# Loads of the cached blocks and the first layer of their compression ahead of the projection

## The chip, the cores and the metric

The kernel runs on 1 core of one Trainium2 chip. The metric is device time in microseconds (us) of one execution; three runs are given for the kernel before. The engines are PE (matrix multiply), DVE (vector), ACT (scalar), POOL (GpSimd) and SP (the queue that issues most transfers). They run in parallel and meet at semaphores.

## What is computed

One layer of a decoder step for a prompt of 512 tokens and 8 sample tokens, 520 columns in all, width 1024:

```
m = silu(c) @ ada_w + b -> shift1, scale1, gate1, shift2, scale2, gate2
h = rmsnorm(x) * (1 + scale1) + shift1
z = h @ w_in                      -> recurrent group, queries, K/V of three branches, gates
past = cache_cmp_kv[page_table]   -> 8 sequences x 8 pages x 128 rows, K and V
hidden = sum over m of chunk_proj(past, w1)[m] + pos @ w1      (first layer)
ck = gelu(hidden) @ w2                                          (second layer)
o = gates * (attend(ck), attend(selected blocks), attend(window))
x += gate1 * concat(rmsnorm(recurrent), rmsnorm(o)) @ w_out
x += gate2 * PEER(rmsnorm(x) * (1 + scale2) + shift2);  y = rmsnorm(x)
```

The change touches the order of m, h, z, hidden and ck for the sample tokens. The formulas stay as they are.

## The kernel before

The engines' programs are written out by hand, one function for each engine; the order of the lines is the order on the engine, and on SP, POOL and ACT it is also the order in which transfers are issued. All tensors of the front section are views of one tile in SBUF, `arena`, so the profile calls most of them by that name.

**Modulation.** The matrix `ada_w` comes as 48 chunks of 512 KB. The first 16 are loaded as four parts of 2048 KB (`load_head`) and used by four wide steps (`ada_step`, L576, 512 columns each). ACT copies each result (`copy_m9`), PE turns it (`turn_m9`, L586), DVE adds the bias (`shift_m`). The other 32 chunks (`load_tail`, two buffers) are used two per piece of the projection, from piece 2 on. In between, PE sums the squares of x that ACT makes (`strip_sums`, L556) and spreads the roots (`spread_roots`, L563).

**Projection.** The loop over n from 0 to 17 (ZC is 18) multiplies one piece of 128 output features: 8 x 2 matmuls of 260 columns (L691), weights of 512 KB in two buffers (`w_in`), results in banks 0 to 3 of `ps`. DVE copies the even pieces and ACT the odd ones (`z_moved`). Piece n + 2's weights are issued when piece n is done (`z_ready`). After pieces 0 and 1 come the gate columns and the bias rows (`gate_strips`, `bias_rows`, `gate_sums`).

**Cached blocks.** `page_rows` reads a page number from SBUF and issues one load of 128 KB (128 rows of 1 KB). 64 loads fill `xpool`: blocks 0 to 19 on SP (8 before the loop, then 4 in each of the rounds 2, 3 and 4), blocks 20 to 63 on POOL, behind a wait for the third wide part. `hidden_pages` (L605) is the first layer, for keys (c = 0) and values (c = 1), 128 matmuls in the trace each, with a position sum of 64 narrow ones (L610). It stands after piece 4. Gelu follows on ACT, then the second layer (`keys_pages`, `values_pages`, L618 and L624), whose last copy piece 6 waits for.

**What else is on the queues.** In round 4 of its loop SP loads the window keys (`win_kT`, 2048 KB), in round 5 the recurrence weights (`wlru`). From round 7 on it loads three selected blocks (`pool_s`) a round into the memory of `xpool`. POOL stores the bias scratch, builds the bias tables through memory (L474 to L486), and then loads 21 selected blocks.

Behind the loop stand the attention over the caches (from L742; the first work is the transposes of L749), the prompt's attention and the feed-forward part, which takes most of the span.

## Time and profile before

| | |
|---|---|
| median of 3 runs | 1851.36 us (1847.32 to 1853.66) |
| the profiled execution's own time | 1851.92 us |
| its span, first to last instruction | 1850.1 us |
| mean granted TensorE clock | 0.963 |
| PE busy | 1755.8 us (95%) |
| DVE, ACT, POOL busy | 1317.2, 646.4, 350.5 us |
| PE's share of the chain that ended last | 83% |
| moved by DMA | 467.88 MB, mean 253 GB/s |

Times in the rows are from the span's start. In a row of a timeline stand the start, the length, the engine, the line, the operation, output<-input, the shape, the count, and in brackets how long the engine had been idle before and what released it. In tables of windows "busy (x)" comes for each engine in turn, then the granted clock of PE as a share of full speed, the mean busy share of the 16 DMA engines, and GB/s. "q1" is the queue of SP, "q0" that of POOL. A landing is the time from issue to the completion of a transfer.

### The profile page before, as it was taken

The numbers are of one execution on the slowest core, as the hardware profiler recorded it, in microseconds if no ns is written. First come the engines' busy times: TensorE is split into PE (matmuls) and PEld (weight loads), VectorE is DVE, ScalarE is ACT, GpSimd is POOL, SyncE is SP. The second block draws the span as 40 slices with busy tenths as digits, with TensorE's granted clock in tenths as the row PEclk, the third lists the DMA queues.
The fourth block names the chain that finished last, engine by engine and source line by source line (L and its number), as shares of the span: only waits on it lengthen the run. The fifth ranks groups of instructions, "written<-read, shape, count | busy, mean of one in ns | idle before, by whom it ended". The sixth has DMA issues, their size and how long they took to land.

```text
span 1850.1 us, 30371 instructions
## 1 busy us (share of the span) xinstructions
PE 1755.8 (95%) x11385; PEld 1633.9 (88%) x11385; DVE 1317.2 (71%) x2982; ACT 646.4 (35%) x1020; POOL 350.5 (19%) x390
## 2 busy tenths in 40 slices
PE   5999998789889999999999999999999999999997
PEld 3868876447789989999899999999999999999997
DVE  2102434663387789999899999994787777777776
ACT  2103422662132233334333343333333333333332
POOL 1512010000000001111233333332222222222220
PEclk8999996799899999999999999999999999999998
DMA  8948572500333226877799999999999999999992
GB/s 299 311 141 267 202 228 78 197 1 1 134 134 94 78 83 243 285 244 225 227 331 355 350 337 342 347 347 358 404 376 340 342 330 342 340 340 335 341 310 76
DMA packets 176606, 467.88 MB, mean 253 GB/s; under 512 B 20457, under 2 KB 90089, under 8 KB 174820
## 3 DMA queue, kind: packets, MB, share of 16 engines
q1 hardware_dynamic: 130532, 290.36, 45.3%
q0 software_dynamic: 45952, 175.97, 26.7%
q8 instruction: 68, 1.11, 0.2%
q14 instruction: 54, 0.44, 0.1%
HBM read 408.89 MB, written 64.17 MB: 256 GB/s over the span
## 4 chain that ended last, share of the span: by engine, by line
PE 83%; DVE 8%; DMA 3%; issue 2%; ACT 2%; POOLq 1%; POOL 0%; SPq 0%; DVEq 0%; ACTq 0%
PE ps L1064 29%; PE ps L960 25%; PE ps L691 5%; PE ps L1045 5%; PE ps L947 4%; PE ps L900 3%; PE ps L605 2%; ACT arena L1107 2%; PE ps L876 1%; PE ps L576 1%; DVE ul L1712 1%; PE ps L868 1%; DVE arena L1589 1%; DMA xT<-in_xT 1%; POOLq L281 1%
## 5 line engine op out<-in xcount | busy, mean ns | idle before, releaser
L1712 DVE TENSOR_TENSOR ul<-raw,uh 128x1024 fp32r<-128x1024 f32 x256 | 311.7, 1223 | 134.7 <-ACT uh L1107 118.2
L960 PE MATMUL ps<-hh,uh 128*128 128x392 f32 x1024 | 359.2, 351 | 5.3 <-DVE ul L1712 5.2
L960 PE MATMUL ps<-hl,uh 128*128 128x392 f32 x1024 | 350.5, 342 | 0.0
L960 PE MATMUL ps<-hh,ul 128*128 128x392 f32 x1024 | 349.5, 341 | 0.0
L1064 PE MATMUL ps<-ah,uh 128*128 128x392 f32 x1000 | 340.0, 340 | 3.0 <-DVE al L1921 3.0
L1064 PE MATMUL ps<-ah,ul 128*128 128x392 f32 x1000 | 342.1, 342 | 0.0
L1064 PE MATMUL ps<-al,uh 128*128 128x392 f32 x1000 | 341.4, 341 | 0.0
L1107 ACT ACTIVATE uh<-raw 128x1024 fp32r<-128x1024 f32 x256 | 270.2, 1055 | 123.8 <-PE ps L1064 103.6
L510 POOL DMA_INDIRECT xT<-in_u,gidx x128 | 147.5, 1152 | 584.8 <-DVE zg L1759 359.8
L510 POOL DMA_INDIRECT xT<-in_v,gidx x128 | 132.6, 1036 | 418.3 <-DVE vacc L1911 384.5
L1107 ACT ACTIVATE zbuf<-ps 128x392 f32<-128x392 f32 x128 | 63.7, 498 | 402.2 <-PE ps L960 355.5
L960 PEld LDWEIGHTS ps<-hh,uh 128*128 128x128 f32 x1024 | 193.9, 189 | 8.3 <-DVE ul L1712 6.6
L960 PEld LDWEIGHTS ps<-hl,uh 128*128 128x128 f32 x1024 | 193.9, 189 | 0.0
L960 PEld LDWEIGHTS ps<-hh,ul 128*128 128x128 f32 x1024 | 193.7, 189 | 0.0
L1064 PEld LDWEIGHTS ps<-ah,uh 128*128 128x128 f32 x1000 | 188.3, 188 | 3.3 <-issue 3.3
L1064 PEld LDWEIGHTS ps<-al,uh 128*128 128x128 f32 x1000 | 188.1, 188 | 0.0
L1064 PEld LDWEIGHTS ps<-ah,ul 128*128 128x128 f32 x1000 | 188.1, 188 | 0.0
L1911 DVE SCALAR_TENSOR_TENSOR vacc<-xT,ag,vacc 128x1024 f32<-128x1024 f32 x127 | 162.4, 1279 | 0.0
L1759 DVE CUSTOM_DVE_ANT_0 xT<-xT,hg 128x1024 f32<-128x1024 f32 x128 | 155.8, 1219 | 5.0 <-DMA xT<-in_u,gidx 5.0
L1107 ACT ACTIVATE ah<-zin 128x392 fp32r<-128x392 f32 x128 | 68.2, 533 | 227.6 <-DVE zin L1918 227.6
L691 PE MATMUL ps<-arena 128*128 128x260 f32 x576 | 135.2, 394 | 3.4 <-DVE arena L1381 2.0
L691 PEld LDWEIGHTS ps<-arena 128*128 128x128 f32 x576 | 111.3, 196 | 21.4 <-issue 4.2
(352 smaller groups left out, 2240.0 us busy)
## 6 DMA issues: line engine op xcount, KB each, us to landing
raw<-in_uT SPq DMA_DIRECT2D x128, 512.0 KB
raw<-in_v SPq DMA_DIRECT2D x128, 512.0 KB
zs<-zbuf SPq DMA_DIRECT2D x128, 196.0 KB
gw<-stage POOLq DMA_DIRECT2D x28, 896.0 KB
gr<-gw SPq DMA_DIRECT2D x32, 784.0 KB, 8.1
zin<-zs SPq DMA_DIRECT2D x128, 196.0 KB
arena<-in_ada_w SPq DMA_DIRECT2D x32, 512.0 KB, 4.6
arena<-in_w_in SPq DMA_DIRECT2D x18, 512.0 KB, 6.3
```

The lines of the kernel that those rows point to most:

```text
L510: pool.indirect_dma_start(out=gb[:, s, :], out_offset=None, in_=table, in_offset=bass.IndirectOffsetOnAxis(ap=gidx[:, n:n + 1], axis=0)).t ...
L605: mm(ps[g * HD:(g + 1) * HD, b + h, 1 - m:257 - m], w1p[:, c * 16 + m * 8 + j, :], xv[:, h, :, c, g, j, :], start=(m == 0 and j == 0), sto ...
L691: last = mm(ps[:, 2 * (n % 2) + h, 0:HALF], win_w[:, (n % 2) * KD + k, :], hT[:, k, h * HALF:(h + 1) * HALF], start=(k == 0), stop=(k == K ...
L900: last = mm(ps[:, 2 + 2 * (c % 3) + h, 0:HALF], wout[:, k, c * P:(c + 1) * P], zT[:, k, h * HALF:(h + 1) * HALF], start=(k == 0), stop=(k ...
L947: last = mm(ps[:, b + h, 0:HALF], weights[w](k), moving[m](k)[:, h * HALF:(h + 1) * HALF], start=(first and n == 0 and w == 0 and m == 0), ...
L960: last = mm(ps[:, bank, 0:DN], w[x][:, k * P:(k + 1) * P], m[:, k, G0:TOK], start=(k == 0 and x == 0 and m is hh), stop=(k == KD - 1 and x ...
L1045: last = mm(ps[:, 4 + n % 4, t * P:(t + 1) * P], oh[:, n % 6, t * P:(t + 1) * P], oh[:, n % 6, (4 + t) * P:(5 + t) * P], start=True, stop= ...
L1064: last = mm(ps[:, dc, 0:DN], w[:, q, cols], m[:, q, :], start=(first and w is uh and m is ah), stop=False)
L1107: return act.activation(out, in_, f, **kw)
L1712: tt(ul[:, i % 4, :], raw[:, i % 4, :], uh[:, i % 4, :].bitcast(F32), SUB).then_inc(S["lo_done"], 1)
L1759: dve.tensor_tensor_reduce(gb[:, n % 4, :], gb[:, n % 4, :], hg[:, :], 1.0, 0.0, MUL, ADD, zg[:, n:n + 1]).then_inc(S["ttr_done"], 1)
L1911: stt(vacc[:, :], gb[:, n % 4, :], ag[:, n:n + 1], vacc[:, :], MUL, ADD).then_inc(S["acc_step"], 1)
```

## The change

The loads of the 64 cached blocks go to three queues and to the start: SP issues 22 to 31 behind the first part and x, and 48 to 63 behind parts 1 and 2; POOL issues 0 to 15 and 32 to 47 from the start, without the wait for the third part; ACT issues 16 to 21 before its first copy. The weights `w1p` and `posp` go ahead of them. The page table is one row on SP, no longer a broadcast on POOL.

The first layer is cut into four pieces (`hidden_half(c, h)`), placed behind parts 0, 1, 2 and 3. The wide parts all use bank 6 and their turns bank 7, since banks 2 to 5 now hold the hidden sums. Gelu of both follows at once on ACT, into two tiles (`hid`, `hid2`). The second layer stands after piece 1, and piece 2 waits for its last copy. SP's loads of selected blocks begin in round 2, three a round; in round 3 SP also waits for the second layer. POOL's order is otherwise as before: scratch, bias tables, 21 selected blocks.

The diff, without the hunks of the list of semaphore names and of two counts that follow from it; lines around the changes are left out:

```diff
@@ -172,7 +172,7 @@
...
         oha = at(39321, OHA_W)
-        hid = at(40345, 546)
+        hid, hid2 = at(40345, 546), at(6800, 512)
         ckT = at(40891, 544)
@@ -291,17 +291,26 @@
...
+            def load_pages(a, b, s):
+                for n in range(a, b):
+                    page_rows(sp, xpool[:, n, :], io["pool_c"], n, s)
+            load(pgi[0:1], io["page_table"], S["page_loaded"])
             load(cT, io["cT"], S["c_loaded"])
...
             load(xT[:, :, :], io["xT"], S["x_loaded"])
+            load(w1p, io["w1p"], S["w1k_loaded"])
+            load(posp, io["posp"], S["w1k_loaded"])
+            sp.wait_ge(S["page_loaded"], 16)
+            load_pages(22, 32, S["half_k"])
             load(par[:, 0:80], io["par"], S["tables_loaded"])
...
             load_head(2, 2)
+            load_pages(48, 64, S["gather_k"])
             sp.wait_ge(S["ada_ready"], 1)
             load_head(3, 0)
-            load(wgate, io["w_gate"], S["wgate_loaded"])
+            load(wgate, io["w_gate"], S["small_loaded"])
             load(oha[0:33], io["oha"], S["buckets_loaded"])
@@ -315,14 +324,6 @@
...
                     load(w2[g * HD:(g + 1) * HD, c, g * HD:(g + 1) * HD], io["cmp_w2"][c], S["w2_loaded"])
-            sp.wait_ge(S["page_loaded"], 16)
-            def load_pages(a, b):
-                for n in range(a, b):
-                    page_rows(sp, xpool[:, n, :], io["pool_c"], n, S["gather_k"])
-            load_pages(0, 8)
-            load(w1p, io["w1p"], S["w1k_loaded"])
-            load(posp, io["posp"], S["pos_loaded"])
@@ -334,12 +335,11 @@
...
                 load(win_w[:, (n % 2) * KD:(n % 2 + 1) * KD, :], io["w_in"][n], w_l[n % 2])
-                if 2 <= n <= 4:
-                    load_pages(4 * n, 4 * n + 4)
-                if n >= 7:
-                    sp.wait_ge(S["hid_ready"], 2)
-                    for m in range(3 * (n - 7), min(3 * (n - 6), 32)):
-                        page_rows(sp, sel[:, m, :], io["pool_s"], m, S["gather_s"])
+                sp.wait_ge(S["hid_ready"], 2)
+                for m in range(3 * (n - 2), min(3 * (n - 1), 32)):
+                    page_rows(sp, sel[:, m, :], io["pool_s"], m, S["gather_s"])
+                if n == 3:
+                    sp.wait_ge(S["ck_ready"], 2)
                 load_tail(2 * n - 4)
@@ -460,18 +460,17 @@
...
             pool.memset(ident[:, :], 0.0).then_inc(S["pool_done"], 1)
-            pool.dma_start(pgi, io["page_table"].to_broadcast([P, NB * PAGES])).then_inc(S["page_loaded"], 16)
             pool.wait_ge(S["pool_done"], 1)
...
             pool.wait_ge(S["page_loaded"], 16)
-            pool.wait_ge(S["ada_ready"], 3)
-            for n in range(20, 64):
+            for n in range(16):
+                page_rows(pool, xpool[:, n, :], io["pool_c"], n, S["half_p"])
+            for n in range(32, 48):
                 page_rows(pool, xpool[:, n, :], io["pool_c"], n, S["pages_k"])
-                if n == 44:
-                    pool.wait_ge(S["act_init"], 3)
-                    pool.dma_start(rscratch, rsb[0:NH]).then_inc(S["scratch_stored"], 16)
+            pool.wait_ge(S["act_init"], 3)
+            pool.dma_start(rscratch, rsb[0:NH]).then_inc(S["scratch_stored"], 16)
             pool.wait_ge(S["scratch_stored"], 16)
@@ -569,81 +568,93 @@
...
-                if i >= 2:
-                    pe.wait_ge(S["m9_ready"], i - 1)
+                bank = 6 if i < ADA_HEAD else 4 + i % 2
+                if i >= 1:
+                    pe.wait_ge(S["m9_ready"], i if i < ADA_HEAD else i - 1)
                 for kk in range(2):
                     for j in range(4):
-                        last = mm(ps[32 * j:32 * j + 32, 4 + i % 2, 0:width], cT[:, 2 * j + kk, :], rhs(2 * j + kk),
+                        last = mm(ps[32 * j:32 * j + 32, bank, 0:width], cT[:, 2 * j + kk, :], rhs(2 * j + kk),
                                   start=(kk == 0), stop=(kk == 1))
...
                 pe.wait_ge(S["m9_ready"], i + 1)
-                if i >= 2:
-                    pe.wait_ge(S["mt_done"], i - 1)
+                bank = 7 if i < ADA_HEAD else 6 + i % 2
+                if i >= 1:
+                    pe.wait_ge(S["mt_done"], i if i < ADA_HEAD else i - 1)
                 m9, n = (mhead, 4) if i < ADA_HEAD else (mtail, 1)
                 for q in range(n):
-                    last = mm(ps[:, 6 + i % 2, q * 9:(q + 1) * 9], m9[:, i % 2, q * P:(q + 1) * P], pick[:, 0:9], start=True, stop=True)
+                    last = mm(ps[:, bank, q * 9:(q + 1) * 9], m9[:, i % 2, q * P:(q + 1) * P], pick[:, 0:9], start=True, stop=True)
                 last.then_inc(S["mt_ready"], 1)
-            def hidden_pages(c):
-                if c == 0:
-                    pe.wait_ge(S["w1k_loaded"], 16)
-                    pe.wait_ge(S["pos_loaded"], 16)
-                    pe.wait_ge(S["gather_k"], 16 * 20)
-                    pe.wait_ge(S["pages_k"], 16 * 44)
-                    pe.wait_ge(S["z_moved"], 4)
-                else:
-                    pe.wait_ge(S["m9_ready"], ADA_HEAD + 6)
-                xv = xpool.rearrange("p (h a) (c g j n) -> p h a c g j n", h=2, c=2, g=2, n=8)
-                b = 2 + 2 * c
-                for h in range(2):
-                    for m in range(2):
-                        for j in range(8):
-                            for g in range(2):
-                                mm(ps[g * HD:(g + 1) * HD, b + h, 1 - m:257 - m], w1p[:, c * 16 + m * 8 + j, :],
-                                   xv[:, h, :, c, g, j, :], start=(m == 0 and j == 0), stop=(m == 1 and j == 7),
-                                   skip_group_check=True)
+            xv = xpool.rearrange("p (h a) (c g j n) -> p h a c g j n", h=2, c=2, g=2, n=8)
+            def hidden_half(c, h):
+                if c == 0 and h == 0:
+                    pe.wait_ge(S["w1k_loaded"], 32)
+                    pe.wait_ge(S["half_k"], 16 * 16)
+                    pe.wait_ge(S["half_p"], 16 * 16)
+                if c == 0 and h == 1:
+                    pe.wait_ge(S["gather_k"], 16 * 16)
+                    pe.wait_ge(S["pages_k"], 16 * 16)
+                for m in range(2):
+                    for j in range(8):
+                        for g in range(2):
+                            last = mm(ps[g * HD:(g + 1) * HD, 2 + 2 * c + h, 1 - m:257 - m], w1p[:, c * 16 + m * 8 + j, :],
+                                      xv[:, h, :, c, g, j, :], start=(m == 0 and j == 0), stop=(m == 1 and j == 7),
+                                      skip_group_check=True)
+                if h == 1:
+                    last.then_inc(S["hid_ready"], 1)
+            def position(c):
                 for mj in range(16):
                     for g in range(2):
-                        last = mm(ps[g * HD:(g + 1) * HD, b, 300:301], w1p[:, c * 16 + mj, :],
-                                  posp[:, c * 16 + mj:c * 16 + mj + 1], start=(mj == 0), stop=(mj == 15))
-                last.then_inc(S["hid_ready"], 1)
+                        mm(ps[g * HD:(g + 1) * HD, 2 + 2 * c, 300:301], w1p[:, c * 16 + mj, :],
+                           posp[:, c * 16 + mj:c * 16 + mj + 1], start=(mj == 0), stop=(mj == 15))
             def keys_pages():
-                pe.wait_ge(S["gelu_ready"], 1)
+                pe.wait_ge(S["gelu_ready"], 2)
                 pe.wait_ge(S["w2_loaded"], 64)
-                pe.wait_ge(S["z_moved"], 5)
+                pe.wait_ge(S["z_moved"], 1)
                 mm(ps[:, 0, 0:512], w2[:, 0, :], hid[:, 0:512], start=True, stop=True).then_inc(S["ck_ready"], 1)
...
             def values_pages():
-                pe.wait_ge(S["gelu_ready"], 2)
                 pe.wait_ge(S["ck_moved"], 1)
                 for b in range(NB):
-                    last = mm(ps[0:NCMP_S, b // 4, (b % 4) * P:(b % 4 + 1) * P], hid[:, b * 64:b * 64 + NCMP_S],
+                    last = mm(ps[0:NCMP_S, b // 4, (b % 4) * P:(b % 4 + 1) * P], hid2[:, b * 64:b * 64 + NCMP_S],
                               w2[:, 1, :], start=True, stop=True)
...
             pe.wait_ge(S["prep_done"], 3)
-            for g in range(ADA_HEAD):
-                if g == 1:
-                    pe.wait_ge(S["act_init"], 2)
-                    for k in range(KD):
-                        last = strip_sums(0, hT, k, KD)
-                    last.then_inc(S["sum_ready"], 1)
-                if g == 2:
-                    pe.wait_ge(S["rstd_ready"], 1)
-                    spread_roots(1, 0)
-                if g >= 1:
-                    turn_m9(g - 1)
+            def head_step(g):
                 pe.wait_ge(head_l[g % 3], 16 * (g // 3 + 1))
...
                 ada_step(g, lambda k: aw[:, :, k, :], 512)
-            turn_m9(ADA_HEAD - 1)
+            head_step(0)
+            turn_m9(0)
+            pe.wait_ge(S["act_init"], 2)
+            for k in range(KD):
+                last = strip_sums(0, hT, k, KD)
+            last.then_inc(S["sum_ready"], 1)
+            hidden_half(0, 0)
+            position(0)
+            head_step(1)
+            pe.wait_ge(S["rstd_ready"], 1)
+            spread_roots(1, 0)
+            turn_m9(1)
+            hidden_half(1, 0)
+            position(1)
+            head_step(2)
+            turn_m9(2)
+            hidden_half(0, 1)
+            head_step(3)
+            turn_m9(3)
+            hidden_half(1, 1)
...
-                pe.wait_ge(S["wgate_loaded"], 16)
+                pe.wait_ge(S["small_loaded"], 80)
                 pe.wait_ge(S["mt_done"], ADA_HEAD)
@@ -680,7 +691,7 @@
...
                     pe.wait_ge(S["z_moved"], n - 1)
-                if n == 6:
+                if n == 2:
                     pe.wait_ge(S["ck_moved"], 2)
@@ -693,31 +704,26 @@
...
                     gate_strips()
+                    pe.wait_ge(S["gelu_ready"], 2)
                     bias_rows()
...
                     pe.wait_ge(S["act_init"], 3)
+                    keys_pages()
                     gate_sums()
+                    values_pages()
                 if 7 <= n <= 13 and n % 2:
                     lru_gate(n, 0)
-                if n == 5:
-                    pe.wait_ge(S["gelu_ready"], 2)
                 if n >= 2:
...
                     lru_gate(n, 1)
-                if n == 5:
-                    values_pages()
                 if n == 2:
...
                         turn_m9(ADA_HEAD + i)
-                if n == 4:
-                    hidden_pages(0)
-                    hidden_pages(1)
-                    keys_pages()
             for i in (30, 31):
@@ -1116,8 +1122,12 @@
...
                     act.wait_ge(S["mt_ready"], i - 1)
-                m9, width = (mhead, 512) if i < ADA_HEAD else (mtail, P)
-                fn(m9[:, i % 2, :], ps[:, 4 + i % 2, 0:width], ACT.Copy).then_inc(S["m9_ready"], 1)
+                bank, m9, width = (6, mhead, 512) if i < ADA_HEAD else (4 + i % 2, mtail, P)
+                fn(m9[:, i % 2, :], ps[:, bank, 0:width], ACT.Copy).then_inc(S["m9_ready"], 1)
+            act.wait_ge(S["page_loaded"], 16)
+            for n in range(16, 22):
+                page_rows(act, xpool[:, n, :], io["pool_c"], n, S["half_k"])
             copy_m9(0)
@@ -1126,19 +1136,12 @@
...
-            def gelu_pages(c):
-                link(fn(hid[:, 0:256], ps[:, 2 + 2 * c, 1:257], ACT.Gelu_apprx_tanh, bias=posb[:, c:c + 1]))
-                fn(hid[:, 256:512], ps[:, 3 + 2 * c, 1:257], ACT.Gelu_apprx_tanh, bias=posb[:, c:c + 1]).then_inc(S["gelu_ready"], 1)
-            def pages_hidden():
-                for c in range(2):
-                    act.wait_ge(S["hid_ready"], c + 1)
-                    link(fn(posb[:, c:c + 1], ps[:, 2 + 2 * c, 300:301], ACT.Copy))
-                    if c == 0:
-                        gelu_pages(0)
-                act.wait_ge(S["ck_ready"], 1)
-                fn(ckT[:, 0:512], ps[:, 0, 0:512], ACT.Copy).then_inc(S["ck_moved"], 1)
-                gelu_pages(1)
+            for c in range(2):
+                act.wait_ge(S["hid_ready"], c + 1)
+                hd = (hid, hid2)[c]
+                link(fn(posb[:, c:c + 1], ps[:, 2 + 2 * c, 300:301], ACT.Copy))
+                link(fn(hd[:, 0:256], ps[:, 2 + 2 * c, 1:257], ACT.Gelu_apprx_tanh, bias=posb[:, c:c + 1]))
+                fn(hd[:, 256:512], ps[:, 3 + 2 * c, 1:257], ACT.Gelu_apprx_tanh, bias=posb[:, c:c + 1]).then_inc(S["gelu_ready"], 1)
@@ -1151,8 +1154,6 @@
...
                     copy_m9(ADA_HEAD + 2 * n - 3)
-                    if n == 4:
-                        pages_hidden()
                     if 8 <= n <= 14:
@@ -1160,6 +1161,9 @@
...
                     continue
+                if n == 1:
+                    act.wait_ge(S["ck_ready"], 1)
+                    fn(ckT[:, 0:512], ps[:, 0, 0:512], ACT.Copy).then_inc(S["ck_moved"], 1)
                 act.wait_ge(S["z_ready"], n + 1)
@@ -1179,7 +1183,7 @@
...
                     copy_m9(ADA_HEAD + 2 * n - 3)
-                if n == 5:
+                if n == 1:
                     act.wait_ge(S["ck_ready"], 2)
@@ -1382,7 +1386,8 @@
...
                 c0, n = (4 * i, 4) if i < ADA_HEAD else (i + 3 * ADA_HEAD, 1)
-                tt(mT[:, c0:c0 + n, :], ps[:, 6 + i % 2, 0:9 * n].rearrange("p (q c) -> p q c", c=9),
+                bank = 7 if i < ADA_HEAD else 6 + i % 2
+                tt(mT[:, c0:c0 + n, :], ps[:, bank, 0:9 * n].rearrange("p (q c) -> p q c", c=9),
                    par[:, ADB + c0:ADB + c0 + n].to_broadcast([P, n, 9]), ADD).then_inc(S["mt_done"], 1)
```

## Rows read from the trace of the kernel before

**Rows 1.** The page: span in 40 slices, and the chain by engine.

```profile
DMA  8948572500333226877799999999999999999992
...
PE 83%; DVE 8%; DMA 3%; issue 2%; ACT 2%; POOLq 1%; POOL 0%; SPq 0%; DVEq 0%; ACTq 0%
```

**Rows 2.** Timeline of PE, 0 to 60 us: start, us, what, count, wait before.

```profile
10.89 3.27 PE L576 MATMUL ps<-arena 128*32 128x512 f32 x16 [10.89 <-DMA arena<-in_ada_w]
19.65 3.85 PE L556 MATMUL ps<-arena,ones 128*32 128x136 f32 x64 [5.50 <-ACT arena L1107]
...
28.90 1.16 PE L563 MATMUL ps<-arena,ident 128*128 128x128 f32 x8 [2.35 <-ACT arena L1107]
...
36.27 1.92 PE L576 MATMUL ps<-arena 128*32 128x512 f32 x16
38.91 1.06 PE L586 MATMUL ps<-arena 128*128 128x9 f32 x8 [0.72 <-ACT arena L1107]
41.95 10.13 PE L691 MATMUL ps<-arena 128*128 128x260 f32 x32 [1.98 <-DVE arena L1381]
```

**Rows 3.** Timeline of PE, 60 to 160 us.

```profile
96.89 16.73 PE L605 MATMUL ps<-arena 128*64 128x256 f32 x128 [4.36 <-DMA arena<-in_pool_c]
113.44 1.99 PE L610 MATMUL ps<-arena 128*64 128x1 f32 x64
115.28 14.02 PE L605 MATMUL ps<-arena 128*64 128x256 f32 x128
...
131.05 1.13 PE L618 MATMUL ps<-arena 128*128 128x512 f32 x2
...
144.05 7.25 PE L691 MATMUL ps<-arena 128*128 128x260 f32 x32 [1.42 <-ACT arena L1107]
```

**Rows 4.** Timeline of SP's queue, 34 to 150 us: start, us, transfer, count.

```profile
41.16 8.16 SPq L282 DMA_DIRECT2D arena<-in_pool_c  x8
...
82.94 0.82 SPq L288 DMA_DIRECT2D arena<-in_ada_w  x2
83.80 0.43 SPq L288 DMA_DIRECT2D xT<-in_win_kT  x1
84.28 0.84 SPq L288 DMA_DIRECT2D arena<-in_w_in  x1
...
94.65 9.76 SPq L288 DMA_DIRECT2D arena<-in_w_in  x1
```

**Rows 5.** The load of in_w_in within 84 to 85 us: its landing.

```profile
DMA to landing us min/median/max: 13.4/13.4/13.4
```

**Rows 6.** Windows: PE, PEld, DVE, ACT, POOL; clock, DMA share, GB/s.

```profile
10.00:16.00 6.00, 3.27 (x16) 0.67 (x16) 0.00 (x0) 0.67 (x2) 0.00 (x0) 1.00 0.99 408
42.00:50.00 8.00, 8.00 (x24) 6.47 (x25) 3.02 (x7) 0.00 (x0) 4.15 (x7) 0.64 0.77 224
52.00:64.00 12.00, 12.00 (x77) 8.88 (x77) 0.70 (x1) 1.44 (x4) 5.52 (x11) 0.86 1.02 362
170.00:230.00 60.00, 59.93 (x474) 50.11 (x473) 27.63 (x94) 27.25 (x42) 0.00 (x0) 1.00 0.59 205
```

**Rows 7.** DMA queues, 83.8 to 97.7 us: packets, MB, share of 16 engines.

```profile
q1 hardware_dynamic: 830, 4.33, 77.3%
q0 software_dynamic: 549, 1.10, 24.5%
```

**Rows 8.** Timelines: POOL from 85 us, then ACT from 15 us.

```profile
87.83 4.19 POOL L478 DMA_DIRECT2D obias<-arena  x8
...
99.45 3.84 POOL L486 DMA_DIRECT2D arena<-obias  x8 [6.89 <-DMA obias<-arena]
...
134.72 0.54 POOL L282 DMA_DIRECT2D arena<-in_pool_s  x1 [0.60 <-issue]
...
15.93 3.67 ACT L1107 ACTIVATE arena<-xT 128x4160 f32<-128x4160 f32 x1 [1.11 <-DMA xT<-in_xT]
```

**Rows 9.** Timeline, 255 to 275 us: the first work behind the projection.

```profile
256.01 1.07 PE L749 MATMUL ps<-ident,arena 128*128 128x128 f32 x8
```

More of the change, by code:

```diff
@@ L780, in _ @@
             hidden_prompt(1, 7, 128)
-            pe.wait_ge(S["w1k_loaded"], 48)
+            pe.wait_ge(S["w1k_loaded"], 64)
             hidden_prompt(0, 1, 160)
```

6 lines of the change are left out of this document (3 added, 3 removed).

## Prediction

> **What bounds the kernel now.** I read the page first. PE carries 83% of the chain that ended last, so time that PE loses in this front section I take as time of the kernel. The same page shows the DMA row at its ceiling in most of the first slices [rows 1]. So the front has two limits that take turns, and the change moves work across the border between them.
>
> Then PE's timeline of the first 60 us [rows 2]: the four wide modulation parts (L576) and their turns (L586), with 10.89, 5.50 and 2.35 us of waiting before them, then projection piece 0 at 41.95. That piece takes 10.13 us where later ones take 7.25 to 7.28: the granted clock was 0.64 over 42 to 50 us [rows 6], that is mostly the lower level (1.2 GHz), after waits of 0.72 and 1.98, and rose to the upper one within the piece.
>
> Then the projection [rows 3]: pieces of 7.25 us; after piece 4 a wait of 4.36 us for the last cached block; the compression's first layer from 96.89 to 131.05; one wait of 1.42 us; then no wait over 0.3 us until L749 at 256.01 [rows 9]. That last start is my ruler: I build its time after the change, and carry the difference one for one to the end.
>
> **What the compression hid.** The loads of SP's queue in the round of piece 4 [rows 4]: two modulation parts (82.94), the window keys of 2048 KB (83.80), projection piece 5 (84.28). Piece 5 landed 13.4 us after its issue [rows 5], at 97.7. PE was ready for it at 92.5, where piece 4's round ended. It did not wait, because 39 us of compression and block waits stood in between. This is the row I trust most.
>
> **Projection start after the change.** The head becomes: part 0, norm sums, half (keys, first blocks), part 1, half (values, first), part 2, half (keys, second), part 3, half (values, second). The first half needs 32 blocks and the layer's weights.
> 1. What must land, by the shapes: c, part 0 and xT (128 + 2048 + 2080 KB) and the weights (1024 + 16 KB), 5.42 MB of long rows; 10 blocks from SP and 6 from ACT, 2.10 MB; and POOL's blocks, one per 1.16 us (0.54 and the idle time of 0.60 before it [rows 8]) from about 4.5 us on, 0.113 MB per us.
> 2. The rate. Long rows alone moved 408 GB/s at a DMA share of 0.99, a stretch with some 40% blocks 362, and blocks nearly alone 224 at a share of 0.77, which is 291 at full share [rows 6]. For this mixture I take 365. The moving starts at 3.0 us, a little earlier than before (the page table is now loaded as one row, no longer broadcast by POOL). From 0.365(T - 3.0) = 7.52 + 0.113(T - 4.5), T = 32. Priced one by one (408 and 291) it is 35. If POOL's blocks beyond the first 16 take no share, 31. Completion comes about 1.3 us after the last byte. I take **34**, bounds 30 and 37.
> 3. The lower bound is not the loads but the norm: xT landed at 15.93 in before; ACT's and POOL's blocks come into its way (0.79 MB and about 10 blocks, 7 us at 291 GB/s), so near 22; square 3.67, sums 3.85 [rows 2, 8] give 30.
> 4. PE from there, at durations of the full clock [rows 2, 3]: four halves of 14.02/2, 28.0; the first starts after a wait, so as the first one of before (16.73 against 14.02) 2.7 more; two position sums of 1.9, 3.8; three parts of 1.92, 5.8; root spreading 1.3; three turns of 1.06 and two of the waits of 0.72 before them, 4.6. Sum 46.2. Projection piece 0 would start at **80.2**.
> 5. Are the other loads in time? Even if SP's queue issues parts 1 and 2 only at 34 (it has blocked at issue before, 9.76 us once [rows 4]), part 1 is there at 41, needed at 45; part 2 at 46, needed at 56; 16 blocks at 1.02 us of issue each [rows 4] by 55, needed at 60; part 3 by 60, needed at 68. No cost. ACT issues its six blocks in some 6 us while it waits for part 0; no cost. The shift of the modulation into piece 0 (1.98 us of waiting for L1381) is hidden behind the last half.
>
> **From the projection start to L749.** Before: 256.01 - 41.95 = 214.1. Leave out the wait 4.36, the compression 34.16, the wait 1.42, and piece 0's slow clock, 10.13 - 7.25 = 2.9, since PE now comes to it without a wait: 171.2. Everything else moves with it unchanged. New waits:
> - Before piece 2: piece 2 now waits for the copy of the compressed values. The nearest row is the 1.42 that piece 6 waited for the same copy in before [rows 3]; now the gates' sigmoids stand ahead of it on ACT too. Bounds 1.4 and 3; I take 1.8.
> - Before piece 5: the transfer is no longer covered. By before's own row PE would be short by 97.7 - 92.5 = 5.2 us. But the company differs. Before, POOL's queue used 24.5% of the DMA engines in the stretch of 13.9 us up to the landing, SP's 77.3% [rows 7]. POOL's order is its compression blocks, the bias scratch, the bias tables (L478 to L486), then 21 selected blocks. The scratch store now waits for the bias matmuls after piece 0 (about 93) and takes 3 us; the tables take 15.5 us, as from 87.83 to 103.3 [rows 8], so to about 112; and the 21 blocks at 1.16 us run until 137. Piece 5's round is at about 120 to 130, right among them: a block of 0.131 MB at 291 GB/s takes 0.45 of every 1.16 us, 38%. SP's 13.9 x 0.773 = 10.7 us of full DMA then take 17.3 in the remaining 62%: 7.8 us short. I take **6.5**, between 5.2 and 7.8.
> - Before piece 6: behind piece 5 in the queue stand three selected blocks, two parts, the recurrence weights and piece 6, 2.2 MB, while each round of PE gives 8.7 us. Before, piece 6 was held at issue for 9.76 us [rows 4] and this too was hidden. Bounds 0 and 6. Either it is late by some us, or the clock is: after waits of 2 and 4.4 us before, 2.9 and 2.7 us were lost. I take 2.7 once.
>
> Sum: 80.2 + 171.2 + 1.8 + 6.5 + 2.7 = 262.4, against 256.0: **6.4 us later**. The profiled execution took 1851.92 (span 1850.1 and 1.8 around it), 0.6 above the median; so 1858.3 by it and 1857.8 by the median; I say 1858.
>
> **Two rules of the Trainium skill.** Blocks are 128 KB each, and their rate is the term that sets T; the rows say 291 GB/s. The Trainium skill, DMA: Bandwidth & Descriptors, section on where the fixed cost comes from, fits a transfer as 2.0 us plus bytes over 436 GB/s, so blocks in a row would lose nothing. By it T would be 26 and 2 more, the norm would bind at 30, and the sum would end at 258.4, 2.4 us later than before, which lies in rival (b). I keep the rows.
> The same page, section "Issuing engines are not separate DMA queues", says that issuing from several engines saves only sequencer time, as all run on the same 16 DMA engines. Against the change: blocks on ACT and POOL come beside SP's only in name. If the queues did add up, SP's own 6.7 MB would land at 22 and the norm would bind, again 4 us less. A DMA share of 0.99 with SP's queue alone at work, from 10 to 16 us, leaves no room for it [rows 6].
>
> **Rivals.**
> (a) Forecast, slower: the uncovered transfer round of pieces 5 and 6. +6.4 us, 1855 to 1867. For it: 97.7 against 92.5. Chance 0.52.
> (b) The two sides cancel: first half at 32, piece 5 short by 5, no second loss. 78.2 + 171.2 + 1.8 + 5.2 = 256.4: 1852. The same comes of a first half at 30 with the waits as in (a): 2.4 us later, 1854. For it: the steady rounds 170 to 230 leave 40% of the DMA free [rows 6], and late rounds slow PE and so the next demand. Chance 0.35.
> (c) Not slower: the loads keep up. SP's long rows win against POOL's blocks, so piece 5 lands as tails do in quiet rounds, and the first half lands at 30. 76.2 + 171.2 + 1.8 = 249.2, 6.8 us gained: 1845. It decides where piece 5 lands within 9 us of its issue. Against it: 13.4 in before, under a lighter POOL. The gain is then what the change is left with: 4.4 + 2.9 of waits and clock at the compression and at piece 0, and the hidden shift. Chance 0.08.
> (d) The interleaving costs clock as well: turns, position sums and narrow parts between the halves let the clock fall, as it did behind the narrow bias matmuls, with PE busy throughout (0.86 over 52 to 64 [rows 6]); two halves pay 2.7 each. +11.8: 1864. Chance 0.05 alone; it also widens (a) upwards.
>
> **Numbers.** A measurement here tells about 0.3%, 5.6 us. Slower by more: most of (a) above 1857, and (d): 0.53. Within: the lower part of (a) and most of (b): 0.36. Faster: (c) and a little of (b): 0.11. Range for 8 in 10: 1848 to 1867; (a) alone: 1855 to 1867.
>
> **What the changed profile would show.** PE's first L605 at 30 to 37, after a DMA wait (right) or at once after the sums (then (c) is likelier). Halves of 7.0 us each, the first near 9.7. Piece 0 at 76 to 84 and 7.25 long. A wait of about 2 us for ACT before piece 2. A wait of 5 to 8 us for in_w_in before piece 5, with POOL's in_pool_s beside it; the next piece slow or waiting. L749 at 256 to 270, and the distance from there to the end as before. Wrong would be: no wait at piece 5; a wait for parts or second blocks between the halves, so that step 5 fails; or a distance behind L749 that changes by more than 1 us.

## The result and the profile after

The changed kernel is slower: 1860.63 us (median of 12 runs, 1850.89 to 1865.32) against 1848.47 us for the kernel before (12 runs, 1843.53 to 1853.66). The ratio is 1.0057, with a 95% interval of 1.0043 to 1.0070, which is about 10.5 us (8 to 13); the two medians lie 12.2 us apart. The profiled execution has a span of 1861.2 us, 11.1 more than before.

The page of the changed kernel: span, PE's busy time, the clock and DMA rows in 40 slices, and the chain by engine.

```profile
span 1861.2 us, 30380 instructions
...
PE 1759.1 (95%) x11385; PEld 1635.6 (88%) x11385; DVE 1317.6 (71%) x2982; ACT 647.1 (35%) x1020; POOL 341.6 (18%) x377
...
PEclk9999996699999999999999999999999999999999
DMA  9487552600243226877799999999999999999982
...
PE 83%; DVE 8%; DMA 3%; ACT 2%; SPq 1%; issue 1%; POOL 0%; DVEq 0%; ACTq 0%; POOLq 0%
```

PE is as busy as before within 3.3 us (1755.8 then) and carries the same share of the chain. The totals say only that PE waited somewhere. The DMA row shows where to look: before it began 8, 9, 4, 8 [rows 1], now 9, 4, 8, 7. In the second slice (47 to 93 us) the DMA engines are busy for less than half as long as before (4 tenths against 9), and in the third for twice as long (8 against 4).

PE's timeline of the head, in the columns of [rows 2]:

```profile
10.53 3.64 PE L576 MATMUL ps<-arena 128*32 128x512 f32 x16 [10.53 <-DMA arena<-in_ada_w]
...
20.58 3.40 PE L555 MATMUL ps<-arena,ones 128*32 128x136 f32 x64 [3.83 <-ACT arena L1113]
30.68 8.55 PE L604 MATMUL ps<-arena 128*64 128x256 f32 x64 [6.71 <-DMA arena<-in_pool_c]
39.05 1.99 PE L614 MATMUL ps<-arena 128*64 128x1 f32 x64
...
45.25 1.16 PE L562 MATMUL ps<-arena,ident 128*128 128x128 f32 x8 [2.35 <-ACT arena L1113]
...
47.37 8.74 PE L604 MATMUL ps<-arena 128*64 128x256 f32 x64
...
61.48 7.13 PE L604 MATMUL ps<-arena 128*64 128x256 f32 x64
...
72.17 7.13 PE L604 MATMUL ps<-arena 128*64 128x256 f32 x64
79.23 7.28 PE L702 MATMUL ps<-arena 128*128 128x260 f32 x32
```

The four pieces of the first layer (L604) stand between the wide parts. PE waits 6.71 us for cached blocks before the first. The first two pieces run 8.55 and 8.74 us, the others 7.13: the clock was at its lower level for part of them, behind the waits of 6.71 and 2.35 us. Piece 0 of the projection starts at 79.23, without a wait and at 7.28 us instead of 10.13 [rows 2].

The same timeline along the projection (L702), against [rows 3] and [rows 9]:

```profile
105.25 7.25 PE L702 MATMUL ps<-arena 128*128 128x260 f32 x32 [1.20 <-ACT arena L1113]
...
123.06 7.28 PE L702 MATMUL ps<-arena 128*128 128x260 f32 x32 [0.74 <-DMA arena<-in_w_in]
130.27 1.08 PE L576 MATMUL ps<-arena 128*32 128x128 f32 x32
...
137.93 9.69 PE L702 MATMUL ps<-arena 128*128 128x260 f32 x32 [6.03 <-DMA arena<-in_w_in]
...
148.92 0.64 PE L576 MATMUL ps<-arena 128*32 128x128 f32 x16 [0.73 <-DMA arena<-in_ada_w]
...
151.77 8.97 PE L702 MATMUL ps<-arena 128*128 128x260 f32 x32 [1.66 <-DMA arena<-in_w_in]
...
162.14 7.26 PE L702 MATMUL ps<-arena 128*128 128x260 f32 x32
...
265.44 1.07 PE L755 MATMUL ps<-ident,arena 128*128 128x128 f32 x8
```

Before had one wait of 1.42 us here, apart from the 4.36 us ahead of the compression. Now PE waits 1.20, 0.74, 6.03, 0.73 and 1.66 us, the last four for transfers, and pieces 5 and 6 run 9.69 and 8.97 us instead of 7.26. L755 (L749 of before) starts at 265.44 instead of 256.01.

SP's queue, against [rows 4]; the second number is how long issuing took:

```profile
26.89 24.42 SPq L282 DMA_DIRECT2D arena<-in_pool_c  x16
...
121.36 0.82 SPq L288 DMA_DIRECT2D arena<-in_ada_w  x2
122.22 0.43 SPq L288 DMA_DIRECT2D xT<-in_win_kT  x1
122.69 0.47 SPq L288 DMA_DIRECT2D arena<-in_w_in  x1
...
132.34 5.28 SPq L288 DMA_DIRECT2D arena<-in_wlru  x2
137.66 5.45 SPq L288 DMA_DIRECT2D arena<-in_w_in  x1
```

The round of piece 5 is the same as before: two parts, the window keys, the weights. Piece 5's weights landed 15.2 us after their issue, at 137.9, which is when PE went on. Before they took 13.4 us [rows 5] and nobody waited. The recurrence weights (L288, `wlru`) and piece 6's weights were held at issue for 5.3 and 5.5 us.

POOL's queue at the same time, against [rows 8]; and the two queues' shares from 122.7 to 137.9 us, against [rows 7]:

```profile
93.31 0.56 POOL L473 DMA_DIRECT2D rscratch<-arena  x1 [52.53 <-ACT arena L1113]
...
107.05 0.59 POOL L282 DMA_DIRECT2D arena<-in_pool_s  x1 [0.27 <-issue]
...
131.06 1.08 POOL L278 DMA_DIRECT2D arena<-in_cmp_w  x2
```

```profile
q1 hardware_dynamic: 779, 3.86, 66.1%
q0 software_dynamic: 501, 1.62, 36.0%
```

POOL's 21 selected blocks run from 107 to 131, and then come two loads of 512 KB, the value weights for the prompt (L278). POOL has 36.0% of the DMA engines where it had 24.5% before, SP 66.1% where it had 77.3%.

Windows ahead of it, in the columns of [rows 6]: the DMA engines are busy for only a fifth of the time while PE works through the last halves and piece 0.

```profile
60.00:80.00 20.00, 18.79 (x164) 12.05 (x165) 5.02 (x14) 3.96 (x8) 0.00 (x0) 1.00 0.22 64
80.00:90.00 10.00, 10.00 (x71) 7.02 (x69) 0.70 (x1) 0.50 (x2) 0.00 (x0) 1.00 0.21 68
```

So 30 us are largely unused, and behind them, from 123 us on, comes the stretch in which PE waits for transfers.

### The profile page after: what moved, and what is told of

It is laid out like the page before. It is cut to its first block, busy times and chain, and to the rows that moved or that the text cites. A ratio compares the mean times of both kernels' runs of the same rounds, so it can differ in the third digit from the quotient of the medians.

```text
span 1861.2 us, 30380 instructions
## 1 busy us (share of the span) xinstructions
PE 1759.1 (95%) x11385; PEld 1635.6 (88%) x11385; DVE 1317.6 (71%) x2982; ACT 647.1 (35%) x1020; POOL 341.6 (18%) x377
## 4 chain that ended last, share of the span: by engine, by line
PE 83%; DVE 8%; DMA 3%; ACT 2%; SPq 1%; issue 1%; POOL 0%; DVEq 0%; ACTq 0%; POOLq 0%
PE ps L1070 29%; PE ps L966 25%; PE ps L702 6%; PE ps L1051 5%; PE ps L953 4%; PE ps L906 3%; PE ps L604 2%; ACT arena L1113 2%; DMA arena<-in_w_in 1%; PE ps L882 1%; PE ps L576 1%; DVE ul L1717 1%; PE ps L874 1%; DVE arena L1594 1%; PE ps L1088 1%
## 5 line engine op out<-in xcount | busy, mean ns | idle before, releaser
L702 PE MATMUL ps<-arena 128*128 128x260 f32 x576 | 136.6, 397 | 9.6 <-DMA arena<-in_w_in 8.4
L702 PEld LDWEIGHTS ps<-arena 128*128 128x128 f32 x576 | 112.0, 197 | 28.3 <-DMA arena<-in_w_in 8.7
```

Source lines behind the costliest of these rows:

```text
L702: last = mm(ps[:, 2 * (n % 2) + h, 0:HALF], win_w[:, (n % 2) * KD + k, :], hT[:, k, h * HALF:(h + 1) * HALF], start=(k == 0), stop=(k == K ...
```

## The experiments

The ruler in all of them is the start of the first matmuls behind the projection: 256.0 us before, 265.4 after. The remaining distance to the end of the span was 1594.1 and 1595.8, and 1590.9 to 1595.8 in the runs below, without a pattern; I take it as noise of about 2 us on a span. The ruler has noise of its own, from the clock in the head: with the same head in PE's program, piece 0 starts at 41.95 in before, 44.51 in e4 and 48.61 in e9, and at 79.23 in the change, 78.74 in e1, 79.28 in e2, 79.15 in e5 and 82.62 in e6. So a ruler from one profile places a loss, and the ratio says whether there is one. Ratios are against the kernel before on the same chips; the medians are not all from the same chip.

| run | ratio (95%) | median us | ruler us |
|---|---|---|---|
| the change | 1.0057 (1.0043 to 1.0070) | 1860.6 | 265.4 |
| e1 keys early | 1.0035 (1.0022 to 1.0048) | 1855.8 | 264.8 |
| e2 blocks late | 1.0005 (0.9986 to 1.0025) | 1851.6 | 258.6 |
| e3 halves behind | 1.0169 (1.0144 to 1.0194) | 1880.2 | 282.0 |
| e4 before, keys in round 5 | 0.9973 (0.9959 to 0.9987) | 1844.6 | 251.5 |
| e5 value weights late | 1.0040 (1.0022 to 1.0058) | 1857.2 | 261.8 |
| e6 keys early, value weights late | 1.0003 (0.9985 to 1.0022) | 1849.0 | 257.1 |
| e7 turns behind the halves | 1.0076 (1.0049 to 1.0104) | 1861.7 | 262.9 |
| e8 the edits of e1, e5, e7, and 10 blocks earlier | 0.9990 (0.9974 to 1.0006) | 1848.5 | 252.8 |
| e9 before, 7 of 8 products left out | one execution | 1831.2 | 237.9 |

The intervals of e2, e4, e6 and e8 lie below that of the change, e3 above it; those of e1, e5 and e7 overlap it.

My theory was that the compression had covered the transfers of pieces 5 and 6, and that once it was gone, the window keys ahead in SP's queue and POOL's selected blocks beside it made them late. The rivals were that only one of the two matters, or neither.

**e1: the window keys before the loop.**

```diff
@@ SP
+            sp.wait_ge(S["h_ready"], KD)
+            load(kwin, io["win_kT"], S["x_loaded"])
             for n in range(2, ZC):
...
-                if n == 4:
-                    sp.wait_ge(S["h_ready"], KD)
-                    load(kwin, io["win_kT"], S["x_loaded"])
```

> The changed kernel with one edit: the window keys (2048 KB) are issued before SP's loop, as soon as the normed x is ready, where the DMA share of the changed kernel is 0.00 (70 to 80 us) and 0.21 (80 to 90), instead of in round 4. My theory (the round of piece 5 lost its cover, and this transfer stands ahead of piece 5's weights): the wait of 6.03 us before piece 5 goes to under 0.5, piece 5 runs at 7.3 instead of 9.69, the wait before piece 6 (1.66) shrinks to under 1; the first work behind the projection moves from 265.4 to 254 to 256, so the kernel lands within 0.3% of the kernel before (ratio 0.997 to 1.002). Rival (POOL's selected blocks alone cost it, the keys' place does not matter): the wait stays at 4 us or more, ratio 1.004 or more.

PE's timeline of this run, from piece 5 on:

```profile
134.42 7.28 PE L701 MATMUL ps<-arena 128*128 128x260 f32 x32 [0.34 <-DMA arena<-in_w_in]
145.29 1.08 PE L575 MATMUL ps<-arena 128*32 128x128 f32 x16 [3.59 <-DMA arena<-in_ada_w]
147.44 1.08 PE L575 MATMUL ps<-arena 128*32 128x128 f32 x16 [1.06 <-DMA arena<-in_ada_w]
...
150.33 9.72 PE L701 MATMUL ps<-arena 128*128 128x260 f32 x32 [0.85 <-DMA arena<-in_w_in]
```

The wait before piece 5 fell from 6.03 to 0.34 us, as expected. But the ruler hardly moved. Most of the waiting turned up one step later, before the two modulation parts of the same round (3.59 and 1.06) and before piece 6 (0.85), 5.5 us where the change has 2.4; piece 6 ran at 9.72 (8.97 in the change), and piece 2 had started 1.1 us later than in the change (106.38 against 105.25), with slow stretches ahead of it. Half of the expectation failed. The ratio says 1.0035, between the two theories. The window of 130 to 148 us in this run:

```profile
130.00:148.00 18.00, 13.00 (x108) 10.31 (x110) 4.66 (x15) 1.11 (x3) 0.88 (x2) 0.92 1.07 225
```

The DMA engines are full (1.07) but move 225 GB/s. That is not the 362 of mixed blocks and long rows [rows 6]. Two things run there: the recurrence weights, in rows of 256 bytes, and POOL's value weights, which go to 64 of the 128 partitions.

**e2: POOL's 21 selected blocks later.**

```diff
@@ POOL
             pool.wait_ge(S["hid_ready"], 2)
+            pool.wait_ge(S["z_moved"], 8)
             for n in range(32, 53):
```

> The changed kernel with one edit: POOL's 21 selected blocks wait until eight pieces of the projection are copied, so its queue is empty around pieces 4 to 6. SP's queue had 66.1% of the DMA engines in the 15.2 us that piece 5's weights took; alone it needs 15.2 x 0.661 = 10.1 us. My theory of the company: the wait before piece 5 falls from 6.03 to about 1 us, the first work behind the projection from 265.4 to 256 to 259, ratio 0.999 to 1.003. Rival (order in SP's own queue alone, POOL's share does not matter): the wait stays at 5 us or more and the ratio at 1.005 to 1.007. Further rival: the late blocks disturb pieces 8 to 10 instead, by 2 us or more.

Piece 5 of this run, and the landing of its weights:

```profile
133.93 9.98 PE L703 MATMUL ps<-arena 128*128 128x260 f32 x32 [2.94 <-DMA arena<-in_w_in]
```

```profile
DMA to landing us min/median/max: 11.1/11.1/11.1
```

The share of SP's queue from 122.7 to 133.8 us, with POOL's queue empty:

```profile
q1 hardware_dynamic: 1044, 4.26, 98.5%
```

The landing fell from 15.2 to 11.1 us with the keys still ahead in the queue, the wait from 6.03 to 2.94 (I had expected about 1), and piece 6 waits no more. This edit takes the blocks and, since they stand behind them, also the value weights out of the stretch, and it gives back 6.8 us of the 9.4 on the ruler; the ratio, 1.0005, agrees. The blocks alone were not moved in any run. The shares carry the size: 15.2 x 0.661 = 10.1 us of full DMA for SP, landed in 11.1. The further rival is small: 1.06 us of waits around 201 us.

**e5: only the value weights later; e6: with the early keys.**

```diff
@@ POOL
+            pool.wait_ge(S["z_moved"], 10)
             load_w1(pool, 1, S["w1v_loaded"])
```

> The changed kernel with one edit: POOL's two loads of the value weights for the prompt (512 KB each, onto 64 partitions), issued at 131 us in the changed kernel right behind its selected blocks, wait until ten pieces are copied. In the run with the early keys the DMA engines stood at a share of 1.0 to 1.1 from 130 to 148 us with only 200 to 270 GB/s, and pieces 5 and 6 waited there. Theory W (these two loads and the recurrence weights are the second half of the loss): the waits of 0.73 and 1.66 us around piece 6 go, its slow clock too, the wait before piece 5 falls from 6.0 to 4 to 5; the first work behind the projection at 259 to 262. Rival (the narrow rows of the recurrence weights alone): nothing changes by more than 1 us.

> The changed kernel with both edits: window keys before SP's loop, and POOL's value weights for the prompt after ten pieces. Theory W: the waits of 3.59, 1.06 and 0.85 us around pieces 5 and 6 that were left with the early keys fall below 1 us in sum and piece 6 runs at 7.3 instead of 9.72; the first work behind the projection at 255 to 258, ratio 0.999 to 1.002. Rival (recurrence weights, 256-byte rows): 3 us or more of waits stay.

In e5 the wait before piece 5 is 5.54 us, above the 4 to 5 expected; those around piece 6 (0.73, 1.66) are gone, and piece 6 runs 7.26. The ruler is at 261.8, 3.7 us back, about what the changed kernel lost at piece 6: 0.73 + 1.66 + 1.7. The ratio does not separate e5 from the change, and in e7 below piece 6 loses 3.2 us less than in the change with the value weights where they were. So e5 alone does not show the 3.7; e6 against e1 is the stronger test, 1.0003 against 1.0035 with intervals that only touch at 1.0022. In e6 no wait over 0.7 us is left behind piece 2, and piece 5 runs 7.26. The same window as above:

```profile
130.00:148.00 18.00, 18.00 (x141) 15.09 (x140) 5.57 (x21) 1.60 (x5) 1.73 (x4) 1.00 0.95 296
```

The share is 0.95 at 296 GB/s, PE is busy for all of the 18.0 us where it was for 13.00 in e1. The recurrence weights and POOL's last blocks were still there, and no wait came with them. The ruler would be at 253.7 were it not for the head, which in this run took 3.4 us longer (first half 10.03, second 8.63, spreading 1.99: clock). The losses of the changed kernel in the projection are thereby put down to three groups of transfers in company: the keys, POOL's blocks and the value weights. Without the last two (e2), or without the first and the last (e6), the kernel is level with before. Moving the keys alone (e1) or the value weights alone (e5) does not do it.

**e9: the cover taken off the kernel before.** The run leaves out 7 of 8 products of the first layer, so its results are not those of the layer.

```diff
@@ hidden_pages
-                        for j in range(8):
+                        for j in range(1):
...
-                                   start=(m == 0 and j == 0), stop=(m == 1 and j == 7),
+                                   start=(m == 0 and j == 0), stop=(m == 1 and j == 0),
```

> The kernel before with 7 of 8 products of the first layer left out (one of the eight row groups of a block is multiplied), so that the compression takes some 7 us instead of 34; every transfer stays. Theory (the compression covered the transfers of pieces 5 and 6): piece 5 stands at about 104 instead of 132, its weights landed at 97.7, so no wait there or under 1 us; but its modulation parts (16.8 us to land, about 108) and piece 6's weights (issued 94.65, held at issue, landed at 112.9 before) now bind: waits of 5 to 8 us in sum before the parts of round 5 and before piece 6, where the kernel before had 1.42. The first work behind the projection at 233 to 237: of 27 us of matmuls taken out only 19 to 23 are gained. Rival (the stretch is free of transfers in need, the loss in the changed kernel comes only from its own early selected blocks): no such waits, and it moves by 27 us to 229.

Pieces 5 and 6 of this run:

```profile
107.53 8.87 PE L691 MATMUL ps<-arena 128*128 128x260 f32 x32
...
123.80 8.97 PE L691 MATMUL ps<-arena 128*128 128x260 f32 x32 [3.96 <-DMA arena<-in_w_in]
```

POOL's first selected block in this run, then the landing of piece 6's weights here (issued at 100.18) and in before (issued at 94.65):

```profile
107.92 0.59 POOL L282 DMA_DIRECT2D arena<-in_pool_s  x1 [0.29 <-issue]
...
DMA to landing us min/median/max: 23.6/23.6/23.6
...
DMA to landing us min/median/max: 18.2/18.2/18.2
```

Matmuls of 26.9 us were taken out (16.73 + 14.02 in [rows 3], less two groups of 1.95). From the first L605 (98.95 here, 96.89 in before) to the ruler it took 139.0 us instead of 159.1: 20.1 gained, 6.7 lost on the way. PE now waits 3.96 us for piece 6's weights, where before it waited 1.42 for ACT, and pieces 5 and 6 run 8.87 and 8.97. The size of the waits is under the 5 to 8 us I had expected (4.0, and 3.3 of clock). The ruler at 237.9 cannot be held against the 233 to 237: the head took 6.7 us longer here, and the wait for the blocks was 0.49 instead of 4.36.

What the wait means is less clear than its sign. POOL's selected blocks wait for the compression, so they too came early, 107.92 instead of 132.38, and ran beside piece 6's weights. PE was ready for piece 6 at 119.8. With the landing of before, 18.2 us, the weights would have been there at 118.4 (an estimate from these rows). So without the compression there is a wait in the kernel before as well, but the rival, that early selected blocks make it, is not ruled out by this run; e2 speaks for their part. One execution was taken, and its size is not safe.

**e3: the four pieces behind all parts.**

```diff
@@ PE
-            hidden_half(0, 0)
-            position(0)
             head_step(1)
...
             turn_m9(3)
+            hidden_half(0, 0)
+            position(0)
+            hidden_half(1, 0)
+            position(1)
+            hidden_half(0, 1)
             hidden_half(1, 1)
```

> The changed kernel with one edit: the four pieces of the first layer stand behind all four wide modulation parts, not between them; all loads stay. Parts 1 to 3 then wait for their loads with nothing to fill the time: part 3 was issued at 51.4 us and lands near 57, so part 3 ends near 60, the compression runs 28 + 4 + 2.7 us and piece 0 starts at 95 to 97 instead of 79.2: 16 to 18 us later, ratio 1.013 to 1.016. If interleaving in halves is worth nothing (rival: the loads of the blocks bind anyway), piece 0 starts at 85 or before, ratio below 1.009.

PE in this run, part 1, part 3 and piece 0:

```profile
40.90 3.64 PE L576 MATMUL ps<-arena 128*32 128x512 f32 x16 [15.49 <-DMA arena<-in_ada_w]
...
59.75 3.29 PE L576 MATMUL ps<-arena 128*32 128x512 f32 x16 [2.69 <-DMA arena<-in_ada_w]
...
96.26 7.28 PE L702 MATMUL ps<-arena 128*128 128x260 f32 x32
```

Piece 0 at 96.26, 17.0 us later than in the change, as expected; the ratio of 1.0169 is a little above the expected 1.013 to 1.016. PE waits 15.49 us for part 1, which SP issued only at 24.63, behind ten blocks (17.28 us of issue). The interleaving is what makes the order of the loads bearable; it is worth 17 us to the change, and it is not what costs the time.

**e7: the halves between part and turn.**

```diff
@@ PE
             head_step(1)
+            hidden_half(1, 0)
+            position(1)
             pe.wait_ge(S["rstd_ready"], 1)
             spread_roots(1, 0)
             turn_m9(1)
-            hidden_half(1, 0)
-            position(1)
             head_step(2)
-            turn_m9(2)
             hidden_half(0, 1)
+            turn_m9(2)
             head_step(3)
-            turn_m9(3)
             hidden_half(1, 1)
+            turn_m9(3)
```

> The changed kernel with one edit in the head of PE's program: each piece of the first layer now stands between a wide part and its turn (part 1, half, root spreading, turn 1, part 2, half, turn 2, part 3, half, turn 3), so that ACT's copy, root and table load run under a half. In the changed kernel the waits before the spreading and the turns are 2.35, 0.72 and 0.72 us, and the half behind the first runs 8.74 instead of 7.13. All four go: 3.8 + 1.6 = 5.4 us; against that turn 3 now stands behind the last half, and the modulation and shift (2 us and one turn) are exposed before piece 0 as in the kernel before: 3 us back. Piece 0 at 76 to 78 instead of 79.2, but possibly at the slow clock (2.9 us more). If the waits of step 4 of the sum are what the head is worth, piece 0 moves by 1.5 to 3 us earlier; ratio 1.004 to 1.006 as the later waits for transfers stay.

The halves and piece 0 of this run:

```profile
30.95 8.76 PE L604 MATMUL ps<-arena 128*64 128x256 f32 x64 [5.41 <-DMA arena<-in_pool_c]
...
43.31 7.13 PE L604 MATMUL ps<-arena 128*64 128x256 f32 x64
...
66.04 7.13 PE L604 MATMUL ps<-arena 128*64 128x256 f32 x64
...
76.14 10.19 PE L702 MATMUL ps<-arena 128*128 128x260 f32 x32 [1.98 <-DVE arena L1385]
```

The waits of 2.35, 0.72 and 0.72 us are gone and the second half runs 7.13. Piece 0 starts at 76.14, 3.1 us earlier, but it now runs 10.19 us at the lower clock behind the exposed shift of 1.98 us, as in before. At piece 1 nothing is left of it (91.20 against 91.38). The ruler is 2.5 us better because piece 6 loses less here (a wait of 0.84, and 7.28 us long); the ratio of 1.0076 (1.0049 to 1.0104) shows no gain and lies above the 1.004 to 1.006 expected. A null result within what can be measured.

**e4: the kernel before with the keys one round later.**

```diff
@@ SP, kernel before
-                if n == 4:
+                if n == 5:
                     sp.wait_ge(S["h_ready"], KD)
                     load(kwin, io["win_kT"], S["x_loaded"])
```

> The kernel before with one edit: the window keys are loaded in round 5 instead of round 4. If this transfer delayed the last cached blocks there (the last one took 9.4 us to land, the median 3.9 us), the wait of 4.36 us before the compression falls to 1 us or less and the kernel gains 3 us and up to 2.7 more where the clock no longer falls: ratio 0.997 to 0.999. Piece 5's weights land near 90 instead of 97.7, and nobody waits for them in either. Rival (blocks bound by POOL's issue, one per 1.16 us to 87.3): the wait stays above 3 us, ratio 1.000. A risk: piece 6's weights land late behind keys and recurrence weights, but piece 6 starts at 144.

The border between the round of piece 4 and the compression:

```profile
94.51 0.59 PE L586 MATMUL ps<-arena 128*128 128x9 f32 x4
95.03 14.03 PE L605 MATMUL ps<-arena 128*64 128x256 f32 x128
```

The wait of 4.36 us [rows 3] is gone, and the first 128 matmuls run 14.03 us instead of 16.73. The ruler is at 251.5, 4.6 us earlier although the head took 2.6 us longer; from piece 0 on it is 7.1 us, which is 4.36 + 2.70. The ratio is 0.9973, clear of 1. This wait and this clock are what the change too takes away at the compression. Here they go by moving one transfer, and the cover stays.

**e8: the change with e1, e5, e7, and 10 of POOL's selected blocks ahead of the bias scratch.** The diff is those of e1, e5 (the value weights) and e7, and:

```diff
@@ POOL
+            pool.wait_ge(S["hid_ready"], 2)
+            for n in range(32, 42):
+                page_rows(pool, sel[:, n, :], io["pool_s"], n, S["pages_s"])
             pool.wait_ge(S["act_init"], 3)
...
-            pool.wait_ge(S["hid_ready"], 2)
-            for n in range(32, 53):
+            for n in range(42, 53):
```

> The changed kernel with four edits: window keys before SP's loop, 10 of POOL's 21 selected blocks ahead of the bias scratch (from 79 us on, where the DMA share is 0.21), its value weights for the prompt after ten pieces, and the halves between part and turn. All transfers that stood around pieces 4 to 6 now lie in the quiet stretch or behind. Theory: no wait over 1 us from piece 3 to the end of the projection, pieces 5 and 6 at 7.3; the first work behind the projection at 250 to 254; ratio 0.995 to 0.999, so a little faster than the kernel before. Rival (the budget of the DMA engines is exhausted anyway): it ends above 257, ratio 1.001 or more.

The ruler is at 252.8, inside the expectation, with no wait over 1.2 us behind piece 0. The ratio is 0.9990 with an interval that holds 1. The change can be brought level with the kernel before; a gain over it is not shown. The lowest ratio of the versions that compute the whole layer is e4's, which has an interval overlapping that of e8.

## Why the prediction was right, by its steps

- **First half at 34, bounds 30 and 37.** Measured 30.68, 3.3 us early. The rate was right: 394 GB/s from 10 to 20 us, 344 from 20 to 30, 375 on average from 3.0 to 29.4, against 365. The amount was not: POOL's queue moved 2.43 MB in that time, where the sum counts 2.8 up to 29.4 and 3.1 up to 32. And I had rounded 33.3 (32 and 1.3) up to 34; for the 1.3 us of completion I gave no row. The norm was far off: x landed in time for the square at 16.86, not near 22, and the norm sums ended at 24.0, not at 30. So it did not bind.
- **From there to piece 0, 46.2.** Measured 48.55. The step that failed is "root spreading 1.3": before it stands a wait of 2.35 us for ACT's copy, table load and root, which [rows 2] showed and which I took as covered by the halves. The root waits for nothing, but ACT reaches it only behind the copy of part 1. In e7, where the spreading stands behind a half, that wait is gone. The second half ran 8.74 instead of 7.0 behind it, rival (d) in small, but in e1 it runs 7.13 behind the same wait, so the wait alone does not bring that on.
- **Piece 0 at 80.2.** Measured 79.23: two misses of opposite sign, so the closeness is luck.
- **Other loads in time.** Right: SP issued part 3 at 51.4 and no part was waited for. Sixteen blocks took 24.4 us of issue instead of 16, and this too was hidden.
- **171.2 for the rest.** Measured 265.4 - 79.2 = 186.2, less waits of 10.4 and slow clock of 4.1: 171.7.
- **Piece 2, 1.8.** Measured 1.20.
- **Piece 5, 6.5 between 5.2 and 7.8.** Measured 6.03. Shares 36% and 66% where the sum had 38% and 62%. The upper bound was worked out wrong: 17.3 us from 83.8, with PE ready at 92.5, is 8.6 short, not 7.8. POOL's blocks ran from 107 to 131, not from 112 to 137.
- **Piece 6 and clock, 2.7.** This is the mis-sized term. Measured: 2.4 of clock at piece 5, 0.73 and 1.66 of waits, 1.7 of clock at piece 6, 6.5 in sum, and 0.74 at piece 4. I had named a late piece 6 or a slow clock and taken one. I had not followed POOL's queue past its selected blocks: the value weights stand there, landing beside piece 6's. Their part is about 3.7 us by e5's profile alone, and by e6 against e1 they have one.
- **Ruler at 262.4.** Measured 265.4, 9.4 us of loss instead of 6.4, and 10.5 us by the ratio. Yet 1858 and the measured 1860.63 lie only 2.6 us apart. That is in part luck: the three runs of before that I could see lay 2.9 us above the median of twelve, which made up for most of a loss put 4 us too small.
- **The two page rules.** The Trainium skill's fit (DMA: Bandwidth & Descriptors, section "Anatomy of one DMA"; it is a fit for transfers that GpSimd issues) gave an estimate of 28 us for the last block, the sum by my rows 33.3; 30.7 lies midway. The rate decides for the rows: 375 GB/s over the stretch, and not 436. Its rule in "Issuing engines are not separate DMA queues" held: in e2, with POOL's queue empty, SP's had 98.5% of the engines instead of 66.1%, and piece 5's weights landed in 11.1 instead of 15.2 us.
- **The last check**, that the distance behind the ruler should not move by over 1 us, failed (it moved by 1.7) and was too strict: it varies by up to 4.9 us between runs that are the same there.

What was argued and not shown: that the clock's fall in each place comes from the wait just ahead of it. The rows show the order of the two, and the second half of e1 (7.13 behind a wait of 2.35) has the wait without the fall. In e9 the clock also fell where PE was busy with the narrow position sums and hardly waited, so waits are not the only thing that goes ahead of it:

```profile
103.00:112.00 9.00, 8.80 (x93) 7.10 (x90) 0.00 (x0) 3.78 (x7) 6.05 (x12) 0.81 0.98 325
```

## What to carry to other kernels

A long stretch of matmuls in a loop is also cover for the transfers issued around it. Before moving it, take the landings of the transfers that fall under it and ask when their users would be due without it; here that was one subtraction, 97.7 against 92.5. Then follow each queue past the point where you stop caring, to the transfer that will arrive in the new company. And when a wait for a transfer has vanished after an edit, look at the next ones: in e1 5.7 us went at piece 5, and in the next round 5.5 us of waits stood where the change has 2.4.

## What the runs showed of the hardware

Full DMA engines can mean very different rates: 394 GB/s for long rows with blocks (10 to 20 us, share 0.99), and 225 GB/s at a share of 1.07 with 256-byte rows and a load onto 64 partitions (e1). Taking the value weights out of the same stretch brought 296 at 0.95, with the 256-byte rows still there (e6); PE no longer waited then, so more long rows were asked for as well, and the part of each is not separated. Issuing on SP is held up too: 1.02 us a block in before [rows 4], 1.6 in the head of the change (16.04 us for ten).
